# Modulation products of eight weight slots gathered in one PSUM bank

## The reference

```python
cond = jax.nn.silu(c)
mod = (cond @ ada_w[l] + ada_b[l])[:, None, :]
sh1, sc1, g1, sh2, sc2, g2 = jnp.split(mod, 6, axis=-1)
h = rmsnorm(x, norm1_g[l]) * (1 + sc1) + sh1
x = x + g1 * hybrid_mixer(h, cos, sin, w_in[l], b_in[l], rel_bias[l], w_branch[l], w_out[l])
h = rmsnorm(x, norm2_g[l]) * (1 + sc2) + sh2
x = x + g2 * swiglu(h, w_ffn_in[l], w_ffn_out[l])
```

## Time and profile before

| | |
|---|---|
| runs: median, lowest, highest | 3759.55, 3758.78, 3766.83 us |
| profiled execution | 3759.26 us, span 3757.9 us |
| granted TensorE clock, mean | 0.983 |
| TensorE busy | 3572.1 us, 95% |
| GpSimd, VectorE, ScalarE busy | 1607.8, 1321.2, 797.4 us |
| chain that ended last | TensorE 88%, VectorE 6%, ScalarE 3% |

### The profile page before, as it was taken

The page is one execution under the profiler, slowest core; times in us unless marked ns, Lnnn a source line. Parts: engine busy times, 40 slices in busy tenths (PEclk is TensorE's granted clock), DMA queues, the critical chain, the costliest instruction groups (busy, mean ns, idle before and its releaser), DMA issues.

```text
span 3757.9 us, 43843 instructions
## 1 busy us (share of the span) xinstructions
PE 3572.1 (95%) x18028; PEld 2757.8 (73%) x18028; DVE 1321.2 (35%) x2254; ACT 797.4 (21%) x1643; POOL 1607.8 (43%) x1020
## 2 busy tenths in 40 slices
PE   6999999999999999999999889889999999979998
PEld 3666677788876666777778677678888887757886
DVE  4733311411147333214111455662111136552113
ACT  2223321100012233211000134421101113331111
POOL 2322346556653223465556522134343343235664
PEclk9999999999999999999999989999999999999999
DMA  6343222333332432224543311013334312113321
GB/s 200 94 128 115 73 71 86 113 101 90 92 99 90 132 115 74 68 89 124 157 135 112 90 45 34 23 47 101 124 100 134 104 56 59 34 48 121 100 91 66
DMA packets 409616, 351.09 MB, mean 93 GB/s; under 512 B 9797, under 2 KB 406853, under 8 KB 409418
## 3 DMA queue, kind: packets, MB, share of 16 engines
q1 hardware_dynamic: 401568, 340.82, 29.2%
q10 hardware_dynamic: 7850, 7.47, 0.8%
HBM read 346.16 MB, written 2.10 MB: 93 GB/s over the span
## 4 chain that ended last, share of the span: by engine, by line
PE 88%; DVE 6%; ACT 3%; issue 1%; DMA 1%; POOL 1%; ACTq 0%; DVEq 0%; POOLq 0%
PE psum L540 26%; PE psum L541 24%; PE psum L542 24%; PE psum L515 2%; PE psum L784 2%; PE psum L892 1%; PE psum L921 1%; DVE psum L1734 1%; PE psum L527 1%; PE psum L717 1%; PE psum L772 1%; PE psum L756 1%; PE psum L758 1%; PE psum L609 1%; DVE k L2205 1%
## 5 line engine op out<-in xcount | busy, mean ns | idle before, releaser
L490 POOL TENSOR_SCALAR weights_hi<-raw_weights 128x1024 fp32r<-128x1024 f32 (+3 forms) x508 | 507.3, 999 | 2079.0 <-PE psum L542 1822.6
L540 PE MATMUL psum<-h_hi,weights_hi 128*128 128x512 f32 (+1 forms) x2896 | 1151.3, 398 | 64.3 <-DVE h_lo L1758 52.9
L493 POOL TENSOR_TENSOR weights_lo<-raw_weights,weights_hi 128x1024 fp32r<-128x1024 f32 (+3 forms) x508 | 1109.4, 2184 | 42.4
L541 PE MATMUL psum<-h_lo,weights_hi 128*128 128x512 f32 (+1 forms) x2896 | 1102.0, 381 | 0.0
L542 PE MATMUL psum<-h_hi,weights_lo 128*128 128x512 f32 (+1 forms) x2896 | 1101.4, 380 | 0.0
L540 PEld LDWEIGHTS psum<-h_hi,weights_hi 128*128 128x128 f32 x2896 | 549.9, 190 | 264.2 <-issue 150.5
L542 PEld LDWEIGHTS psum<-h_hi,weights_lo 128*128 128x128 f32 x2896 | 550.0, 190 | 112.3
L541 PEld LDWEIGHTS psum<-h_lo,weights_hi 128*128 128x128 f32 x2896 | 550.7, 190 | 103.6 <-issue 7.9
L540 PE MATMUL psum<-hidden_hi,weights_hi 128*128 128x512 f32 (+1 forms) x1120 | 411.9, 368 | 0.0
L541 PE MATMUL psum<-hidden_lo,weights_hi 128*128 128x512 f32 (+1 forms) x1120 | 411.6, 367 | 0.0
L542 PE MATMUL psum<-hidden_hi,weights_lo 128*128 128x512 f32 (+1 forms) x1120 | 411.2, 367 | 0.0
(11 more groups left out here) (259 smaller groups left out, 3701.6 us busy)
## 6 DMA issues: line engine op xcount, KB each, us to landing
raw_weights<-in_ada_w SPq DMA_DIRECT2D x96, 1024.0 KB, 5.3
raw_weights<-in_w_mlp SPq DMA_DIRECT2D x64, 1024.0 KB, 5.4
raw_weights<-in_w_in SPq DMA_DIRECT2D x56, 1024.0 KB, 5.2
raw_weights<-in_w_ffn_in SPq DMA_DIRECT2D x88, 512.0 KB, 5.1
raw_weights<-in_w_in SPq DMA_DIRECT2D x34, 512.0 KB, 4.6
raw_weights<-in_w_out SPq DMA_DIRECT2D x16, 1024.0 KB, 4.9
raw_weights<-in_w_ffn_out SPq DMA_DIRECT2D x16, 1024.0 KB, 5.0
raw_weights<-in_w_branch SPq DMA_DIRECT2D x56, 128.0 KB, 2.3
```

Of the source, the lines that this page charges most:

```text
L490: gpsimd.tensor_scalar(whi[:, r, c0:c1], raw[:, raw_slot, c0:c1], 1.0, 1.0, ALU.mult, ALU.mult).then_inc(*split_hi.up(*key, half))
L493: gpsimd.tensor_tensor(wlo[:, r, c0:c1], raw[:, raw_slot, c0:c1], whi[:, r, c0:c1].bitcast(F32), ALU.subtract).then_inc(*split.up(*key, half))
L540: tensor.matmul(out, sh, mh, start=first, stop=False, skip_group_check=shared)
L541: tensor.matmul(out, sh, ml, start=False, stop=False, skip_group_check=shared)
```

## The change

The slots of a group are cut into rounds of at most eight. `cond` has 53 columns instead of 32, zeros but for the three vectors at columns 21 to 23. Slot c of a round takes the 32 columns from 21 - 3c on as its stationary part, so its three rows of sums come out on partitions 3c to 3c+2 of each column group and the other slots get zeros added. All slots of a round add up in one bank: only the first product of a column group in the round starts it. ScalarE copies once a round, and the two turning products run once a round, with 24 moving columns. Two turning products of a round are issued behind the first slot of the next one, or at the group's end. VectorE adds the bias from the columns in their new order. To make room, the bf16 identity and causal mask, and the inputs of `cond`, move to areas that are used again later, and `gate` holds four places instead of six; the other two are in the context columns of `X`.

```diff
--- before.py
+++ after.py
@@ -124,9 +124,15 @@
+def ada_rounds(group):
+    return [group[at:at + ROUND] for at in range(0, len(group), ROUND)]
 ADA = ada_groups()
-ADA_BANKS = {"start": ((0, 1), 2), "norm1": ((4, 5), 6), "norm2": ((4, 5), 6), "rope": ((6,), 7), "A": ((6,), 7),
-             "B": ((6,), 7), "feed": ((6,), 7), "gm": ((6,), 7), "up2": ((6,), 7)}
+ADA_BANKS = {"start": (0, 2), "norm1": (4, 6), "norm2": (4, 6), "rope": (6, 7), "A": (6, 7), "B": (6, 7), "feed": (6, 7),
+             "gm": (6, 7), "up2": (6, 7)}
+ROUND = 8
 TILES2 = {0: (("q", 1), ("k", 1), ("u", 3), ("u", 2)), 1: (("q", 2), ("k", 2), ("v", 1), ("p", 3)),
@@ -320,12 +326,8 @@
     ident, perm, meanm, dup, dupperm, sel = (cst[:, n, :] for n in range(6))
-    identb = top.take("identity_bf16", [P, P], BF16)
-    causal = top.take("causal_bf16", [P, P], BF16)
     eps = top.take("eps", [P, 1])
-    cond = top.take("cond", [P, KT, 32])
-    cond_in = top.take("cond_in", [P, 3, KT])
-    cond_sigmoid = top.take("cond_sigmoid", [P, 3, KT])
+    cond = top.take("cond", [P, KT, 32 + 3 * ROUND - 3])
     mod = top.take("mod", [P, 48, 3])
@@ -333,6 +335,8 @@
     one = Map(nc, top.at)
+    identb = one.take("identity_bf16", [P, P], BF16)
+    causal = one.take("causal_bf16", [P, P], BF16)
     hh = one.take("h_hi", [P, KT, T], F32R)
@@ -347,6 +351,8 @@
     cm = tmp1.take("causal_f32", [P, P])
+    cond_in = tmp1.take("cond_in", [P, 3, KT])
+    cond_sigmoid = tmp1.take("cond_sigmoid", [P, 3, KT])
     pos = tmp1.take("pos_int", [P, T], I32)
@@ -370,7 +376,7 @@
     work_out = Map(nc, gat.at).take("squares_out", [P, 3, T])
-    gate = gat.take("gates", [P, 6, T])
+    gate = gat.take("gates", [P, 4, T])
     ffn = Map(nc, one.at)
@@ -451,8 +457,10 @@
     def gate_place(jj, g):
+        if jj and g < 4:
+            return gate[:, g, :].rearrange("p (a n) -> p a n", a=2)
         if jj:
-            return gate[:, g, :].rearrange("p (a n) -> p a n", a=2)
+            return X[:, 2 * g - 8:2 * g - 6, 0:TC]
         return X[:, 2 * g:2 * g + 2, 0:TC] if g < 4 else staging_c[:, g - 4, :].rearrange("p (a n) -> p a n", a=2)
@@ -500,35 +508,43 @@
         def ada_steps(name, l=None):
-            group = ADA[name if l is None else (name, l)]
-            banks, cols = ADA_BANKS[name]
-            n = len(group)
-            for c in range(n + 2):
-                if c < n:
-                    bk, (layer, j) = banks[c % len(banks)], group[c]
+            rounds = ada_rounds(ADA[name if l is None else (name, l)])
+            bk, cols = ADA_BANKS[name]
+            def columns(r):
+                layer, j = rounds[r][-1]
+                tensor.wait_ge(*ada_moved.at(layer, j))
+                if r == 0:
+                    tensor.wait_ge(*free[cols])
+                for h in range(2):
+                    at = 3 * ROUND * (2 * r + h)
+                    ins = tensor.matmul(bank[cols][:, at:at + 3 * ROUND], ada_rows[:, r % 2, h * P:h * P + P],
+                                        sel[:, 0:3 * ROUND], start=r == 0 and h == 0,
+                                        stop=r == len(rounds) - 1 and h == 1, skip_group_check=True)
+                ins.then_inc(*ada_col.up(layer, j))
+                for slot in rounds[r]:
+                    ada_col.note(*slot)
+            for rnd, slots in enumerate(rounds):
+                for c, (layer, j) in enumerate(slots):
                     r = slab["ada", layer, j][0]
                     tensor.wait_ge(*arrived[r].at("ada", layer, j))
-                    tensor.wait_ge(*free[bk])
+                    if c == 0:
+                        tensor.wait_ge(*free[bk])
+                    at = 3 * (ROUND - 1 - c)
                     for kk in range(2):
                         for g in range(4):
-                            ins = tensor.matmul(bank[bk][32 * g:32 * g + 32, 0:256], cond[:, 4 * kk + g, :],
-                                                view[:, 4 * kk + g, :], start=kk == 0, stop=kk == 1,
-                                                tile_position=(0, 32 * g))
+                            ins = tensor.matmul(bank[bk][32 * g:32 * g + 32, 0:256], cond[:, 4 * kk + g, at:at + 32],
+                                                view[:, 4 * kk + g, :], start=c == 0 and kk == 0,
+                                                stop=c == len(slots) - 1 and kk == 1, tile_position=(0, 32 * g))
                     ins.then_inc(*ada_row.up("ada", layer, j))
-                    free[bk] = ada_moved.at(layer, j)
-                if c >= 2:
-                    layer, j = group[c - 2]
-                    tensor.wait_ge(*ada_moved.at(layer, j))
-                    if c == 2:
-                        tensor.wait_ge(*free[cols])
-                    for h in range(2):
-                        at = (2 * (c - 2) + h) * 3
-                        ins = tensor.matmul(bank[cols][:, at:at + 3], ada_rows[:, (c - 2) % 2, h * P:h * P + P],
-                                            sel[:, 0:3], start=c == 2 and h == 0, stop=c == n + 1 and h == 1,
-                                            skip_group_check=True)
-                    ins.then_inc(*ada_col.up(layer, j))
-                yield
+                    if c == 0 and rnd:
+                        columns(rnd - 1)
+                    yield
+                free[bk] = ada_moved.at(*slots[-1])
+            columns(len(rounds) - 1)
+            yield
             free[cols] = mod_done.at(name, l)
@@ -1154,18 +1170,15 @@
         def ada_steps(name, l=None):
-            group = ADA[name if l is None else (name, l)]
-            banks, cols = ADA_BANKS[name]
-            n = len(group)
-            for c in range(n + 2):
-                if 1 <= c <= n:
-                    layer, j = group[c - 1]
-                    bk, q = banks[(c - 1) % len(banks)], (c - 1) % 2
-                    scalar.wait_ge(*ada_row.at("ada", layer, j))
-                    if c >= 3:
-                        scalar.wait_ge(*ada_col.at(*group[c - 3]))
-                    scalar.copy(ada_rows[:, q, :], bank[bk][:, 0:256]).then_inc(*ada_moved.up(layer, j))
-                yield
+            bk, cols = ADA_BANKS[name]
+            for r, slots in enumerate(ada_rounds(ADA[name if l is None else (name, l)])):
+                for _ in slots:
+                    yield
+                scalar.wait_ge(*ada_row.at("ada", *slots[-1]))
+                scalar.copy(ada_rows[:, r % 2, :], bank[bk][:, 0:256]).then_inc(*ada_moved.up(*slots[-1]))
+                for slot in slots:
+                    ada_moved.note(*slot)
+            yield
@@ -1691,26 +1704,28 @@
         for n in range(3):
-            vector.tensor_tensor(cond[:, :, n], cond_in[:, n, :], cond_sigmoid[:, n, :],
+            vector.tensor_tensor(cond[:, :, 3 * (ROUND - 1) + n], cond_in[:, n, :], cond_sigmoid[:, n, :],
                                  ALU.mult).then_inc(*dve_misc.up("cond"))
         def ada_finish(name, l=None):
-            group = ADA[name if l is None else (name, l)]
+            rounds = ada_rounds(ADA[name if l is None else (name, l)])
             cols = ADA_BANKS[name][1]
-            vector.wait_ge(*ada_col.at(*group[-1]))
-            at, n = 0, len(group)
-            while at < n:
-                (layer, j0), end = group[at], at + 1
-                while end < n and group[end] == (layer, j0 + end - at):
-                    end += 1
-                j1 = j0 + end - at
-                for m in range(3):
-                    ins = vector.tensor_tensor(
-                        mod[:, 2 * j0:2 * j1, m],
-                        bank[cols][:, 6 * at:6 * end].rearrange("p (n m) -> p n m", m=3)[:, :, m],
-                        ada_bias[:, layer, 2 * j0:2 * j1], ALU.add)
+            vector.wait_ge(*ada_col.at(*rounds[-1][-1]))
+            for r, slots in enumerate(rounds):
+                at, n = 0, len(slots)
+                found_columns = bank[cols][:, 6 * ROUND * r:6 * ROUND * r + 6 * ROUND].rearrange(
+                    "p (h c m) -> p c h m", h=2, m=3)
+                while at < n:
+                    (layer, j0), end = slots[at], at + 1
+                    while end < n and slots[end] == (layer, j0 + end - at):
+                        end += 1
+                    j1 = j0 + end - at
+                    for m in range(3):
+                        ins = vector.tensor_tensor(
+                            mod[:, 2 * j0:2 * j1, m].rearrange("p (c h) -> p c h", h=2), found_columns[:, at:end, :, m],
+                            ada_bias[:, layer, 2 * j0:2 * j1].rearrange("p (c h) -> p c h", h=2), ALU.add)
                     ins.then_inc(*mod_done.up(name, l))
-                at = end
+                    at = end
@@ -2336,7 +2351,7 @@
     for g in range(4):
-        sel[32 * g, 0] = sel[32 * g + 1, 1] = sel[32 * g + 2, 2] = 1.0
+        sel[32 * g + np.arange(3 * ROUND), np.arange(3 * ROUND)] = 1.0
```

## The result

The changed kernel took 3731.07 us (median of 4 runs, 3724.64 to 3735.19), the kernel before 3763.19 (median of 4 on the same chip, 3758.78 to 3771.25). The ratio is 0.9911, with a 95% interval of 0.9885 to 0.9937. The forecast was 3723, in a range of 3711 to 3738. The profiled execution of the changed kernel took 3724.64 us with a span of 3723.2, 34.6 under that of before, where 36.7 had been added up. That the total is so near is in part luck: the term for attention came out 4.7 us larger than forecast and the one for the index stage 3.3 us smaller, and a third that had been put at nothing costs 4 to 6 us.

A forecast was written before the change was run, and what follows sets the result against it. TensorE, busy for 95% of the span and 88% of the chain, was taken as the bound; savings of 15.0 + 18 + 3.3 + 0.9 less 0.5 made 36.7 us off a median of 3759.55, so about 3723, range 3711 to 3738.

The forecast's parts named there:

- the term for attention: Attention A and B, two layers: fewer turning pairs and waits for ScalarE's copy save 18 us.
- the one for the index stage: Rope group beside the index selection, two layers: net 1.7 us saved in each, 3.3 together.
- a third that had been put at nothing: Memory map: two gate places moved into the residual's context columns were said to cost 0.
- the dense stages: Feed, gm and up2: turning pairs taken out save 4.4, 2.9 and 7.7 us, 15.0 in sum.
- 24 columns instead of 3: the lower end: Wider turning product: cost between 0 (one issue floor) and 0.9 us for 18 pairs; the middle, 0.5, was taken.
- the full sum: A and B, two layers: 12.9 us of pairs plus 8.0 of waiting, 20.9 us saved.
- the 18 taken: A and B: 18 us counted out of the full 20.9, with the softmax chain expected to be late next.
- the softmax chain: A and B: late next, as TensorE already waits 1.2 us for ScalarE's exponentials; half the full sum, 10.4, was the lower end.
- Rope: Stage beside the index selection: two 1.13 us waits go, part returns at the pair; 3.3 us saved in two layers.
- The remaining lone pair of gm2: Second gm group: a turning pair that stands alone goes, worth 0.53 us.
- The start: Start: the last copy waits for its slot alone, not for a pair, saving 0.9 us.
- The rival that attention keeps half of what it is given: A, B and rope: softmax chain takes half of TensorE's gain, late weights all of rope's; 3734 us, chance 0.17.

The follow-up runs named there:

- its repeat: The changed kernel run again unedited, beside the kernel before with only the new memory map: 3728.9 us, ratio to before 0.9911.
- the best addresses: Pads put first-stack `h` and second-stack `hidden` 128 past a multiple of 256: kernel before 3739.15 us, changed kernel 3705.85 us.
- the map alone: The kernel before with only the changed kernel's memory map; slots, copies and turning products as before: 3765.97 us, ratio 1.0012.
- waits put back: The changed kernel with 78 ScalarE copies of constants put back and the next slot waiting for each, no turning pairs: 3744.82 us.
- the two shifted ones of before: The kernel before with 32 bytes ahead of both stacks' areas, 3737.86 us, and with 32 bytes ahead of the first stack's alone, 3739.15 us.
- the slots one tile earlier: The changed kernel with rope's slots and copies one tile earlier, its pair one tile later: 3724.51 us; the same with addresses set to the best seen: 3696.5 us.
- as put back: The changed kernel with 78 turning pairs put back on constants, results unused, no copies or waits for them: 3755.92 us, 27.0 over the changed kernel.

## Why the prediction was right, step by step

**The mechanism and the dense stages: right.** 18 pairs and 18 copies are left, and the slots of up2 stand at even distances except at a round's pair. The changed kernel in order of time, up2 and then a pair in feed:

```profile
2634.98 1.07 PE L538 MATMUL psum<-raw_weights,cond 128*32 128x256 f32 x16
...
2644.49 1.07 PE L538 MATMUL psum<-raw_weights,cond 128*32 128x256 f32 x16
...
2654.03 1.07 PE L538 MATMUL psum<-raw_weights,cond 128*32 128x256 f32 x16
...
1895.41 1.07 PE L538 MATMUL psum<-raw_weights,cond 128*32 128x256 f32 x16
...
1907.81 1.07 PE L538 MATMUL psum<-raw_weights,cond 128*32 128x256 f32 x16
1908.81 0.62 PE L521 MATMUL psum<-constants,ada_rows 128*128 128x24 f32 x4
...
1920.65 1.07 PE L538 MATMUL psum<-raw_weights,cond 128*32 128x256 f32 x16
```

The steps of up2 are 9.51 and 9.54 us here and up to 9.63 further on (9.64 was forecast, from the earlier trace rows). In the table's two rows from feed to gm2 the gain is 14.1 us, where the sum has 14.4 for the same stretches. The remaining lone pair of gm2 falls into the last stretch, where the memory map covers it.

**24 columns instead of 3: the lower end.** In feed the step is 12.40 us without a pair and 12.84 with one of 24 columns, so 0.44 against the 0.43 of 3 columns; 0.5 us had been set aside and at most 0.2 is there. The Trainium skill, "TensorE: Matmul & The Clock Gate", "Back-to-back issue gap", puts all widths up to 64 at one floor; on this point the trace agrees (0.44 against 0.43). The record itself is longer (275 ns against 262), but that is not the distance.

**A and B: the full sum, not the 18 taken.** 10.9 us a layer from A's first to B's last slot, 21.7 in both, against 19.8 for the full sum without B's last pair, which stands behind that stretch; 0.8 of the surplus is the pair's wait in A, the rest is open. I had kept back 2.9 us for the softmax chain. It took nothing: TensorE waits 1.2 us for exponentials ahead of A's first slot and 1.2 us for their sums behind A's last unit, each once and as long as before. The first is in the earlier trace rows, the second is this line of before (228 to 425):

```profile
PE psum L758 <- DVE softmax_stats L1938: 1.2, 1, 1.2
```

The waits of the changed kernel, A (224 to 310) and then B (311 to 412):

```profile
PE psum L771 <- ACT softmax_buffers L1334: 1.2, 1, 1.2
PE psum L774 <- DVE softmax_stats L1953: 1.2, 1, 1.2
```

```profile
PE psum L521 <- ACT ada_rows L1178: 0.9, 1, 0.9
```

In A the pair waits for nothing (0.4 was forecast), in B 0.94. Behind B, up to the norm's slot, the first layer gained 2.5 us and the second lost 0.6, with the same instructions in both layers. Here the granted clock differs: before loses 1.7 us to a fall at 426 to 430 that the changed kernel hasn't, and in the second layer the changed kernel loses 3.4 (1434 to 1444) where before loses 1.7 (1460 to 1464). The changed kernel and its repeat take 300.6 us for this stretch with no fall, 303.6 where falls take 3.4 away and 305.0 where they take 5.1.

**Rope: 3.3 predicted, nothing came.** This is the step that failed. The forecast went: two waits of 1.13 gone ahead of the slot that frees the raw buffer, a wait of some 2.5 us for split weights near 183, and 1.13 at the pair. All three are there in the first layer, and the weights land 2.44 us earlier behind the group's first slot (20.50 us against 22.94):

```profile
177.69 1.05 POOL L498 TENSOR_SCALAR weights_hi<-raw_weights 128x1024 fp32r<-128x1024 f32 x1 [8.22 <-DMA raw_weights<-in_w_in]
```

```profile
181.23 0.50 PE L556 MATMUL psum<-h_hi,weights_hi 128*128 128x512 f32 x1 [2.14 <-POOL weights_lo L501]
...
189.67 0.62 PE L521 MATMUL psum<-constants,ada_rows 128*128 128x24 f32 x4 [1.04 <-ACT ada_rows L1178]
...
1202.63 0.50 PE L556 MATMUL psum<-h_hi,weights_hi 128*128 128x512 f32 x1 [3.44 <-POOL weights_lo L501]
```

What the step left out is what such an idle can do to the clock. Before had its idle time in four pieces of 0.43 to 1.13 us, and the granted clock stayed at 1.00. Now the largest piece is 2.14 us, and behind it the granted clock is at 0.50, TensorE's lower level of 1.2 GHz. Busy time by engine, then the granted clock, the share of DMA and GB/s, in stretches of 2 us, before and then changed:

```profile
184.00:186.00 2.00, 2.00 (x11) 1.64 (x12) 2.00 (x9) 0.00 (x0) 1.92 (x3) 1.00 0.38 70
186.00:188.00 2.00, 1.56 (x8) 0.95 (x6) 2.00 (x8) 0.00 (x0) 2.00 (x2) 1.00 1.08 385
188.00:190.00 2.00, 2.00 (x9) 1.65 (x10) 1.97 (x3) 0.00 (x0) 1.92 (x3) 1.00 0.65 163
```

```profile
182.00:184.00 2.00, 2.00 (x8) 1.54 (x7) 2.00 (x7) 0.00 (x0) 1.92 (x2) 0.69 0.85 298
184.00:186.00 2.00, 2.00 (x6) 1.61 (x5) 2.00 (x6) 0.00 (x0) 1.92 (x3) 0.50 0.10 10
186.00:188.00 2.00, 2.00 (x9) 1.55 (x9) 1.97 (x8) 0.00 (x0) 1.92 (x3) 0.96 0.89 252
```

The missing share adds up to 0.62 + 1.00 + 0.08 = 1.7 us. The stage gained 0.7, so at most 2.4 without the fall. In the second layer the weights land only 1.1 us earlier behind the group's first slot, the wait is 3.44, and another fall, at 1203 to 1207, takes 1.7: the stage lost 0.7 and would have gained at most 1.0. Without the two falls that makes up to 3.4 us, the forecast. One pair of traces shows it without a fall: at the best addresses, in the first layer, the stage takes 72.57 us in the kernel before and 71.05 in the changed one, and neither has a fall in it. That is 1.5 us, where 1.7 a layer was forecast. The fall is not certain at that place. Over all profiled executions it stands there in 10 of 12 stages where the slots' waits are merged and the slots left in place (two layers of six kernels), in 3 of 10 where the waits are apart (before, the map alone, waits put back, the two shifted ones of before), and in none of 4 with the slots one tile earlier, in which the stage is 4.5 to 5.3 us shorter. In these four a fall of 3.4 to 17 us stands at the head of A instead, as in 7 of the other 22. Moving the slots is an experiment on the wait; that the falls are what is missing of the 3.3 us is read from the rows, one execution of each kernel, and was not tried by itself.

**The start: 0.9 predicted, 0.8 found, which is within the spread.** ScalarE's copy waits for its slot and not for a pair, and begins 1.6 us earlier (40.20 against 41.76); VectorE works on the norm's columns from 45.06 and not from 46.37, and its next instruction starts at 45.86 and not at 46.45. At norm1's slots and at the first rope slot 0.8 us are left. In this execution of the changed kernel the granted clock is 0.50 from 19 to 60 us, in that of before it is 1.00 there. Over all profiled executions the stretch takes 155.8 to 158.7 us, kernels of both kinds mixed, so 0.8 us can't be told from nothing here.

**The memory map: put at nothing, costs 4.5 us.** I had looked at who reads and writes the moved arrays, and not at what the move does to the addresses of everything behind them. The map alone costs 4.5 us by the ratio, and the last stretch of 340 us carries 5.0 of the 6.0 us between the profiled spans. It took `hidden` of the second stack from 128 past a multiple of 256 to 96 past one.

**The sum.** Dense came as forecast as far as it can be seen apart, A and B 21.7 against 17 up to B's last slot, rope 0 against 3.3, start 0.8 against 0.9, the map -4.5 against 0. The change without its map, by medians on one chip each, is 37.1 us at the changed kernel's addresses, 34.6 at those of before (3762.61 against 3728.01, the changed kernel with 32 bytes ahead of both maps) and 33.3 at the best ones; these don't differ by more than the runs allow. 36.7 less 4.5 for the map is 32.2, and the medians lie 32.1 apart, which is closer than the interval of the ratio (10 us either way) lets one read. The range held the time. The rival that attention keeps half of what it is given (3734) lies closer to the median than the forecast (3731.07 against 3723), and is refuted all the same: attention gave everything.

## What to carry to other kernels

Where one engine carries nine tenths of the chain, count what each instruction adds to the distance of its neighbours' starts in a stage without waits, not its record: that made 78 pairs worth 27 us, as put back. When waits on the bounding engine are merged or moved, look at how long the one left over is, since the clock fell behind one long wait far more often than among several short ones (10 of 12 stages against 3 of 10, one execution of each kernel). And a change that moves arrays is to be compared with a kernel that only moves them, or what is measured may be the addresses: 25 us came here from 32 bytes.

## What the runs showed of the hardware

The pace of back-to-back products depends on where their moving rows start in SBUF. 32 bytes more ahead of everything brought the kernel before from 3762.61 to 3737.86 us (0.9932, 0.992 to 0.9945). Products of 512 columns follow each other at 0.227 to 0.229 us, as a mean over a stack, where the moving rows start 128 past a multiple of 256 bytes, and at 0.232 to 0.234 us at the remainders 0, 32, 64, 96 and 160. The split weights stand ahead of both maps and moved in no run, and in one stretch of one execution the two paces stand side by side with the same weight buffers (before, last stretch: `h` at 96 with 0.233, `hidden` at 128 with 0.227). So it is the moving rows, and this is why the two stacks seem to answer unlike: their arrays behind `h` have other remainders. It adds up, as an estimate: some 4500 products of `h` in the first stack, 5 ns closer, are 23 us, and the profiled span of the kernel before with 32 bytes ahead of `one` alone is 22.0 us shorter. Why 128 and not 0, and why 256 columns go another way, is open; `h` never stood at 0 or 32, and 192 and 224 were not run for any array.

Falls of the granted clock to 0.50 come behind idles of 1.2 us in some executions and stay out behind idles of 2.36 in others (the changed kernel at the better addresses, first layer's rope stage). A fall of 3.4 us takes 1.7 away, and one at the head of A in the second layer lasted some 17 us, with TensorE at work, and took 8.5.
